# Softmax weights of the mixers: the division by the sums moved from VectorE to ScalarE, the reciprocals to GpSimd

## The reference

```python
def token_mixer(h, w_in, conv_w, conv_b, gate_bias, mlstm_norm_gain, w_out):
    aq, ak, av, mq, mk, mv, mo, mg = split(h @ w_in)
    # attention half: 8 heads of 64, three dilated windows mixed by their log-denominators
    aq = partial_rotary(split_heads(aq, 8), positions) * 64 ** -0.5
    ak = partial_rotary(split_heads(ak, 8), positions)
    attn_out = merge_heads(dilated_attention_mixture(aq, ak, split_heads(av, 8)))
    # mLSTM half: 4 heads of 128, depthwise convolution of width 5 and silu on q and k
    mq, mk = split(silu(depthwise_conv(concat(mq, mk), conv_w) + conv_b))
    cell = mlstm(mq, mk, mv, gates) + mlstm_backwards(...)
    mlstm_out = sigmoid(mo) * rms_norm(cell) * gain
    return concat(attn_out, mlstm_out) @ w_out
```

## Time and profile before

| | |
|---|---|
| median of 3 runs | 2072.3 us (2072.22 to 2072.38) |
| the profiled execution's own time | 2072.22 us |
| its span, first to last instruction | 2070.4 us |
| granted TensorE clock | 0.999 |
| busy: PE, DVE, ACT, POOL | 98%, 81%, 49%, 5% |
| the chain that ended last, by engine | PE 90%, DVE 6%, ACT 2%, issue 1% |

### The profile page before, as it was taken

One profiled execution on the slowest core, in us unless ns is written; L12 is line 12 of the kernel. 1 busy time (PEld: TensorE's weight loads), 2 busy tenths in 40 slices (PEclk: granted clock), 3 DMA queues, 4 the chain that ended last, 5 costly groups with the idle time before them and its releaser, 6 DMA issues.

```text
span 2070.4 us, 26673 instructions
## 1 busy us (share of the span) xinstructions
PE 2037.6 (98%) x10290; PEld 1721.4 (83%) x10290; DVE 1670.9 (81%) x2798; ACT 1016.0 (49%) x1204; POOL 109.5 (5%) x237
## 2 busy tenths in 40 slices
PE   7999999999999999999999999999999999999998
PEld 6988878888978888988888889788888888878887
DVE  5788888886579886788889876989888887788986
ACT  4454445445554444454454445754445444575442
POOL 0010011000010000000010000010001000001000
PEclk9999999999999999999999999999999999999999
DMA  8577655756446656565566656346666755535662
GB/s 278 163 233 229 199 172 194 226 188 204 154 144 210 201 185 199 164 227 187 200 203 218 197 178 209 123 148 218 193 194 204 231 185 193 177 118 185 192 198 87
DMA packets 291022, 393.77 MB, mean 190 GB/s; under 512 B 9924, under 2 KB 257044, under 8 KB 290768
## 3 DMA queue, kind: packets, MB, share of 16 engines
q1 hardware_dynamic: 284032, 368.22, 54.9%
q10 hardware_dynamic: 4032, 14.68, 2.1%
q0 software_dynamic: 2832, 9.17, 1.6%
HBM read 390.96 MB, written 2.12 MB: 190 GB/s over the span
## 4 chain that ended last, share of the span: by engine, by line
PE 90%; DVE 6%; ACT 2%; issue 1%; POOL 0%; DMA 0%; SPq 0%; POOLq 0%; ACTq 0%; DVEq 0%
PE psum L554 27%; PE psum L556 27%; PE psum L555 26%; PE psum L584 2%; PE psum L581 2%; PE psum L588 2%; DVE w_lo L1508 2%; PE psum L677 1%; DVE conv_tmp L1596 1%; ACT squares L1165 1%; DVE mqk L1596 1%; DVE Y L1535 0%; DVE X L1993 0%; DMA raw<-in_conv_w_in 0%; PE psum L722 0%
## 5 line engine op out<-in xcount | busy, mean ns | idle before, releaser
L1508 DVE TENSOR_TENSOR w_lo<-raw,w_hi 128x2048 fp32r<-128x2048 f32 x349 | 794.7, 2289 | 139.2 <-ACT w_hi L1139 136.2
L1139 ACT ACTIVATE w_hi<-raw 128x2048 fp32r<-128x2048 f32 x349 | 663.1, 1908 | 119.5 <-PE psum L556 78.6
L554 PE MATMUL psum<-w_hi,xT 128*128 128x512 f32 (+1 forms) x1424 | 552.4, 388 | 1.0 <-DVE xT L1688 1.0
L556 PE MATMUL psum<-w_hi,xT 128*128 128x512 f32 (+1 forms) x1424 | 549.1, 386 | 0.0
L555 PE MATMUL psum<-w_lo,xT 128*128 128x512 f32 (+1 forms) x1424 | 549.0, 386 | 0.0
L1559 DVE STREAM_TRANSPOSE h_turned<-h_full 32x128 f32<-32x128 f32 x1408 | 426.2, 303 | 21.1
L554 PEld LDWEIGHTS psum<-w_hi,xT 128*128 128x128 f32 x1424 | 267.5, 188 | 57.3 <-issue 2.9
L556 PEld LDWEIGHTS psum<-w_hi,xT 128*128 128x128 f32 x1424 | 267.5, 188 | 54.1
L555 PEld LDWEIGHTS psum<-w_lo,xT 128*128 128x128 f32 x1424 | 267.6, 188 | 53.3
L554 PE MATMUL psum<-w_hi,h_hi 128*128 128x512 f32 x768 | 299.5, 390 | 0.0
L556 PE MATMUL psum<-w_hi,h_lo 128*128 128x512 f32 x768 | 298.9, 389 | 0.0
(11 more groups left out here) (224 smaller groups left out, 1638.8 us busy)
## 6 DMA issues: line engine op xcount, KB each, us to landing
raw<-in_ffn_w_in SPq DMA_DIRECT2D x176, 512.0 KB, 4.9
raw<-in_ffn_w_gate SPq DMA_DIRECT2D x88, 512.0 KB, 4.0
raw<-in_ffn_w_up SPq DMA_DIRECT2D x88, 512.0 KB, 5.0
raw<-in_ffn_w_down SPq DMA_DIRECT2D x44, 1024.0 KB, 4.9
raw<-in_ffn_w_out SPq DMA_DIRECT2D x44, 1024.0 KB, 4.9
raw<-in_conv_w_in SPq DMA_DIRECT2D x20, 1024.0 KB, 5.4
raw<-in_mix_w_in SPq DMA_DIRECT2D x16, 1024.0 KB, 5.5
raw<-in_mix_w_in SPq DMA_DIRECT2D x24, 512.0 KB, 4.8
```

The costliest lines, as they stand in the source:

```text
L554: pe.matmul(dst, l_hi, r_hi, start=first, stop=False, skip_group_check=loose)
L556: return pe.matmul(dst, l_lo, r_hi, start=False, stop=last, skip_group_check=loose)
L1139: return act.activation(dst, source, ACT.Copy, **kw)
L1508: dve.tensor_tensor(w_lo[u % LO_RING][:], raw[u % LO_RING][:], f32(w_hi[hi_slot[u]][:]), ALU.subtract).then_inc(lo_ready, 1)
```

## The change

`attn_weights` is taken out of DVE's program. POOL gets a loop over the eight heads: it waits for `ex_ready`, raises the two sums to the power of -1 (the exponent is a constant in two unused columns of `mean`), and signals the new `inv_ready`. ACT gets `divided(hd)`: it waits for `inv_ready` and copies the two halves of the weights onto themselves with a scale per partition, and signals `a_ready`. It does this for both heads right behind the two `exps` of its units 5, 7, 9 and 11, so in unit 5 ahead of the exponential of `floor`, and in units 7 and 9 ahead of the `decays`.

```diff
--- before.py
+++ after.py
@@ -247,6 +247,7 @@
         minus_half = sb("minus_half", [P, 8])
         ssum = sb("ssum", [P, 8])
         mean = sb("mean", [P, 8])
+        minus_one = mean[:, 4:6]
         rstd = sb("rstd", [P, 8])
 
 
@@ -414,6 +415,7 @@
         lg_done = sem("lg_done")
         mx_ready = sem("mx_ready")
         ex_ready = sem("ex_ready")
+        inv_ready = sem("inv_ready")
         a_ready = sem("a_ready")
         at_done = sem("at_done")
         at_ready = sem("at_ready")
@@ -1320,6 +1322,13 @@
                                            bias=a_max[:, hd % 3, h:h + 1], accum_out=a_sum[:, hd % 3, h:h + 1])
                     e.then_inc(ex_ready, 1)
 
+                def divided(hd):
+
+                    act.wait_ge(inv_ready, seen.next(inv_ready))
+                    for h in range(H):
+                        e = copy(a_prob[hd % 3][:, h, :], a_prob[hd % 3][:, h, :], scale=a_inv[:, hd % 3, h:h + 1])
+                    e.then_inc(a_ready, 1)
+
                 def heads_result(j):
 
                     act.wait_ge(pv_done, seen.next(pv_done))
@@ -1397,6 +1406,8 @@
                     if n in (5, 7, 9, 11):
                         exps(n - 5)
                         exps(n - 4)
+                        divided(n - 5)
+                        divided(n - 4)
                     if 7 <= n < 11:
                         decays(2 * (n - 7))
                         decays(2 * (n - 7) + 1)
@@ -1844,14 +1855,6 @@
                                                        ALU.add, ALU.min, a_max[:, hd % 3, h:h + 1])
                     ins.then_inc(mx_ready, 1)
 
-                def attn_weights(hd):
-                    dve.wait_ge(ex_ready, seen.next(ex_ready))
-                    b = a_prob[hd % 3]
-                    link(dve.reciprocal(a_inv[:, hd % 3, :], a_sum[:, hd % 3, :]))
-                    for h in range(H):
-                        ins = dve.tensor_scalar(b[:, h, :], b[:, h, :], a_inv[:, hd % 3, h:h + 1], None, ALU.mult)
-                    ins.then_inc(a_ready, 1)
-
                 def low_part(c, source):
                     dve.wait_ge(xt_hi, seen.next(xt_hi))
                     dve.tensor_tensor(xT_lo[:, c, :], source, f32(xT_hi[:, c, :]), ALU.subtract).then_inc(xt_ready, 1)
@@ -1875,8 +1878,6 @@
                         running_maxima()
                     if n == 5:
                         stabilisers()
-                        attn_weights(0)
-                        attn_weights(1)
                     if 3 <= n < 7:
                         rotary_position(n - 3)
                     if 9 <= n < 13:
@@ -1901,9 +1902,6 @@
                         attn_logits(1)
                         for d in range(2):
                             mask_exponents(d)
-                    if n in (7, 9, 11):
-                        attn_weights(n - 5)
-                        attn_weights(n - 4)
                     if n in MIX_CONV_UNITS[:-1]:
                         q_or_k_conv(MIX_CONV_UNITS.index(n))
 
@@ -2092,6 +2090,7 @@
 
 
             link(pool.memset(minus_half[:], -0.5))
+            link(pool.memset(minus_one, -1.0))
             for h in range(H):
                 norm(2 + h)
             set_margins(stages[0])
@@ -2103,8 +2102,13 @@
                     for hd in range(4):
                         pool.wait_ge(osq_ready, seen.next(osq_ready))
                         rstd_of(o_sum[:, hd % 2, :], o_mean[:, hd % 2, :], o_rstd[:, hd % 2, :], W, ors_ready)
+                    seen.skip(ex_ready, 8)
                 elif st["kind"] == "mix":
                     decay_exponents()
+                    for hd in range(8):
+                        pool.wait_ge(ex_ready, seen.next(ex_ready))
+                        pool.tensor_tensor(a_inv[:, hd % 3, :], a_sum[:, hd % 3, :], minus_one,
+                                           ALU.pow).then_inc(inv_ready, 1)
                     pool.wait_ge(cell_ready, seen.next(cell_ready))
                     rstd_of(cell_sum[:], cell_mean[:], cell_rstd[:], P, cell_scaled)
                 new = None if st is stages[-1] else stages[st["n"] + 1]
```

## The result

| | median | lowest to highest | runs |
|---|---|---|---|
| before | 2072.28 us | 2072.13 to 2072.44 | 8 |
| after | 2078.79 us | 2077.38 to 2078.98 | 8 |

The ratio is 1.003 (95% interval 1.0021 to 1.0038): 6.5 us slower, outside the forecast range of 2071.7 to 2077.5 (2074.6 was forecast). The profiled execution of after took 2078.81 us, with a span of 2076.9.

The account below looks back on a forecast made before the run. The prediction took TensorE as the bound, busy 2037.6 of 2070.4 us. ScalarE's lateness of +1.5 less 0.37 for small gaps gave +1.1 us a stage, +2.3 for two: 2072.3 to 2074.6 us, range 2071.7 to 2077.5.

Parts of the forecast that it names:

- unit 8: First mixer, ScalarE's decays to silus: conv_out 1.5 us later, TensorE waits 3.7 us, goes on at 1320.4, not 1318.93.
- What VectorE is rid of, and ScalarE's copies: Mixer divisions: VectorE sheds 1.64 us for the first pair of heads, about 1.4 later; ScalarE's copies add 1.62 a pair.
- GpSimd waits out one VectorE operation: Mixers: a pow meeting a VectorE operation with two SBUF inputs ends 0.55 us behind it; 2074.6 us, chance 0.57.
- no-stall rival: Mixers: the pow is not held up, ScalarE is 0.17 us late, a stage gains 0.2; 2071.9 us, chance 0.15.
- the one in which GpSimd gets no turn: Convolution behind the w_lo: back-to-back VectorE operations shut GpSimd out, ScalarE 5.0 us late; 2081.5 us, chance 0.13.
- the one with a further turn lost: Mixers: GpSimd loses one more turn for each pow, +2.4 - 0.37 us a stage; 2076.4 us, chance 0.12.
- The silu 1.5 us late, the gap 3.7, the gap 1.4, the small gaps closed: First mixer: silu 1.5 us late; TensorE's gaps 3.7 before key-query products, 1.4 before head 2's transposes, two small ones gone.
- The sum without the clock: Both mixers: +1.5 - 0.37 = +1.1 us a stage, +2.3 for two; TensorE's clock had no term.
- The pool stage: GpSimd's start: the constant's memset takes 0.1 us while GpSimd waits anyway; forecast 0 before the first mixer.
- The end of the program: Behind VectorE's last instruction: forecast 0 us of added time.
- The small gaps: First mixer: TensorE's waits of 0.17 and 0.20 us before two sums, for VectorE's cell work, close: -0.37.
- Faster: Mixers: VectorE's path alone bound, four gaps closed give 8.1 us, 2064.2; conv_out limits gain to 0.8; chance 0.03.

Follow-up runs that it names:

- e1: The changed kernel with 26 extra matrix products that nothing reads, issued by TensorE before each mixer's first key-query products: 2074.42 us.
- e3: The changed kernel with GpSimd's pow replaced by a memset to a constant, the true reciprocals left out: 2075.57 us.
- e10: The changed kernel with a constant memset for GpSimd's pow and 26 unread matrix products before each mixer's first key-query products: 2071.40 us.
- e5: The kernel before with only GpSimd's extra memset of the constant -1 at the start: 2072.71 us.
- e9: The changed kernel with ScalarE's decays and silus reordered as in e7, and the constant's memset moved from the start to before each mixer: 2068.20 us.
- e4: The kernel before with two extra linked copies of 128x512 on ScalarE ahead of the decays in each mixer: 2074.55 us.
- e8: The kernel before with ScalarE's new order of decays and silus, the divisions still on VectorE: 2072.18 us.
- e7: The changed kernel with ScalarE reordered so that decays of heads not yet due no longer stand ahead of the silus: 2069.09 us.
- e2: The changed kernel with ScalarE's divisions of heads 2 to 7 placed behind the decays of the same unit: 2074.68 us, on two levels.
- e6: The changed kernel with divisions of heads 2 to 7 behind the decays, and 13 unread matrix products before the first key-query products: 2071.62 us.

## Why the prediction was wrong

The step that failed is unit 8: "TensorE, 0.8 us early, waits for it about 3.7 us where it waited 1.40, and goes on at 1320.4 in place of 1318.93." The wait is right (3.7). That TensorE then goes on as before was taken for granted. It goes on at half its clock for 3 to 7 us, and that costs 4.4 us over both mixers (after less e1; 4.2 by e3 less e10). I priced a gap by its length, and named no rival in which the clock takes part, though the windows view prints the granted clock beside each busy time. The Trainium skill (TensorE: Matmul & The Clock Gate, Why this matters for your kernels) warns of idle gaps between bursts of matrix products, behind which the clock is back at half rate. The traces agree, with 0.57 and 0.52 behind the gaps of 3.7 us.

The other steps, one by one:

- *What VectorE is rid of, and ScalarE's copies*: right. Four copies stand in the profile at 1.71 us with their overlap; 1.62 was taken.
- *GpSimd waits out one VectorE operation*: right, with the end of the pow 0.55 us behind that of the subtraction, and idle time of 1.36 us on ScalarE (1.5 forecast). e10 against e1 measures it: 3.0 us over both mixers. The no-stall rival and the one in which GpSimd gets no turn are out by the timeline; so is the one with a further turn lost, by which the pow of head 2 would end at 1309.6: it ended at 1309.32, less the 0.49 of the later start 1308.83 (1308.81 forecast).
- *The silu 1.5 us late, the gap 3.7, the gap 1.4, the small gaps closed*: right, 1.46, 3.7, 1.4 and none.
- *The sum without the clock*: +2.3 forecast, +2.2 measured by e1. That they agree is luck, since three of its terms were wrong:
  - The pool stage stood at nothing ("The extra memset of the constant is 0.1 us at the start, where GpSimd waits for the first sums anyway"); e5 shows 0.54.
  - The end of the program stood at nothing, too. Behind VectorE's last instruction every kernel with the change, other than e9, takes 3.4 us, where before, e4, e5, e8 and e9 take 3.1.
  - The small gaps were taken at 0.37 a mixer. By the starts of TensorE's instructions in e1 and e10 against before, closing them gives 0.85: 0.35 and 0.36 at the two sums, the rest at the products right behind each. The idle time in brackets is counted from the end of the product ahead, which is 0.39 us long where the next one can start after 0.23, so it shows less than the gap costs.

  So without the clock a mixer costs 0.6 us and not 1.1, and with the stall gone too (e10) it is 0.85 us faster than before. The bound of 0.8 us over both stages, which the rival "Faster" puts on any gain, rests on the same 0.37 and was too low.
- *Faster is out, since conv_out can't come earlier*: right for this change. e3, with no stall, has the silus at the old time to 0.1 us. e7 shows the reserve lay in ScalarE's order.

The account of the 6.5 us is thus: 4.4 the clock, 3.0 the stall of GpSimd's reads, 0.5 the shift in the pool stage, 0.3 at the end of the program, and -1.7 what the relieved VectorE gives. The terms overlap in this order of removal: e2, where the stall is hidden without filling, gets only part of the clock back.

The gain that was sought exists. e8 against e9 shows that neither half gives it alone: the new order with the divisions on VectorE gains nothing, the move without the new order loses 6.5 us, both together gain 3.1 (e7), and 4.1 with the constant set later (e9).

## What to carry to other kernels

When work moves from one engine to another, follow the receiving engine's own timeline to the next thing it releases: a queue without a gap hands every microsecond on, however low its share of the span. A longer wait of TensorE must be priced by its length and by the clock behind it; two waits of 2.3 and 1.4 us were cheaper here than one of 3.7, also because a wait that follows can take up what the low clock behind the first one costs (e5, e8). So a change that closes the first of two gaps can lose time. And what GpSimd reads should not fall due while VectorE runs a long operation on two SBUF inputs; put other work of the waiting engine there.

## What the runs showed of the hardware

- Gaps of TensorE and the clock behind them: at 0.6 to 0.8 us it fell in no profiled execution (e1, e6, e10: one level of time, but for one run of e1 at 2075.03, whose mean clock reads 1.0; nor in e7 and e9, with gaps of up to 1.53), at 2.2 and 2.33 us it fell in one mixer of the profiled execution and the times spread over 3.3 and 1.9 us, at 2.7 us three runs of eleven were over 2 us longer, at 3.7 us it fell in both mixers in the profile. One of 2.3 us in the first mixer of e5 was followed by 0.59 too, at no cost: TensorE came 1.5 us late to its next wait, the one of 1.4 for the silu, which is gone there.
- GpSimd's instruction that reads SBUF (pow of 128x2) ended 0.54 to 0.55 us behind the VectorE subtraction it met, all six times in after; the memset in its place, which only writes, took 0.10 us under the same subtraction. VectorE wasn't slowed: the subtraction took 2.29 us as before, and the `pool_y` operation that began at 306.75 under GpSimd's rstd in the kernel before took its 0.69.
- One memset of 0.1 us in GpSimd's program at the start moved the kernel by 0.54 us at a place 300 us later (e5). With the loop of pows as well, GpSimd's last two semaphore instructions stand 0.38 us apart in place of 0.09, which is the 0.3 us at the end; with the memset moved (e9) both are gone. One pause that moves with the number of instructions ahead of it would explain the two; no run shows the pause by itself.
